# Moving the modulation products of a two-layer transformer kernel to VectorE, and attention splits to GpSimd

## What is computed

```python
def modulation(cond, w_mod, b_mod):            # cond (1024,), w_mod (1024, 6144)
    return jnp.split(jax.nn.silu(cond) @ w_mod + b_mod, 6, axis=-1)

h   = x * (1.0 + sc1) + sh1                    # then a mixer, then
x   = layer_norm(ALPHA * x + gt1 * o, ...)
h   = x * (1.0 + sc2) + sh2                    # then a gated feed-forward
x   = layer_norm(ALPHA * x + gt2 * f, ...)
```

## Time and profile before

| | |
|---|---|
| median of three runs | 2785.85 us (2783.92 to 2786.07) |
| the profiled execution | 2784.94 us, its span 2782.8 us |
| busy share of the span | PE 97%, DVE 50%, ACT 36%, POOL 2% |
| window attention of layer 0 | 126 to 240 us |
| first feed-forward, gate/up of the first half | 495 to 693 us |
| its down tiles; its second half | 693 to 795 us; 795 to 973 us |
| heads of differential attention, 17 us each | 1249 to 1380 us |

### The profile page before, as it was taken

The page is one execution under the profiler, slowest core; times in us unless marked ns, Lnnn a source line. Parts: engine busy times, 40 slices in busy tenths (PEclk is TensorE's granted clock), DMA queues, the critical chain, the costliest instruction groups (busy, mean ns, idle before and its releaser), DMA issues.

```text
span 2782.8 us, 41495 instructions
## 1 busy us (share of the span) xinstructions
PE 2704.5 (97%) x17620; PEld 2230.9 (80%) x17620; DVE 1383.0 (50%) x2453; ACT 1014.9 (36%) x1636; POOL 66.7 (2%) x54
## 2 busy tenths in 40 slices
PE   7999999999999999999999999999989999999999
PEld 5876678888888887877788888887766887888887
DVE  3377544434344535427757636459567434433333
ACT  3355543322112227536634323342256222332221
POOL 2000000100000001000001002000000000000000
PEclk9999999999999999999999999999989999999999
DMA  6332010222433331210012332311310223222322
GB/s 263 114 119 70 26 39 31 76 101 93 141 130 113 112 100 54 66 56 8 1 62 77 105 107 91 107 59 64 116 57 9 99 98 95 80 91 88 110 85 89
DMA packets 67351, 236.64 MB, mean 85 GB/s; under 512 B 7392, under 2 KB 10592, under 8 KB 66528
## 3 DMA queue, kind: packets, MB, share of 16 engines
q1 hardware_dynamic: 66592, 231.38, 24.5%
q10 hardware_dynamic: 576, 2.62, 0.3%
HBM read 231.87 MB, written 2.10 MB: 84 GB/s over the span
## 4 chain that ended last, share of the span: by engine, by line
PE 90%; DVE 6%; ACT 2%; issue 1%; DMA 1%; SPq 0%; DVEq 0%; ACTq 0%
PE PSA L695 87%; PE PSA L1010 2%; PE PSA L1281 1%; DVE stat L3197 1%; DVE WS L2363 1%; DMA Y<-in_early 1%; DVE Y L3188 0%; DMA W<-in_weights 0%; PE PSA L1635 0%; ACT WS L1736 0%; DVE HS L2540 0%; ACT Y L2205 0%; DVE YS L2363 0%; DVE PSA L3196 0%; DVE X L2478 0%
## 5 line engine op out<-in xcount | busy, mean ns | idle before, releaser
L695 PE MATMUL PSA<-HS,WS 128*128 128x512 f32 (+1 forms) x6480 | 1300.8, 361 | 11.1 <-DVE HS L2540 5.1
L695 PEld LDWEIGHTS PSA<-HS,WS 128*128 128x128 f32 x6480 | 1091.4, 189 | 209.3 <-issue 12.1
L2363 DVE TENSOR_TENSOR WS<-W,WS 128x1024 fp32r<-128x1024 f32 (+2 forms) x313 | 357.6, 1145 | 622.7 <-ACT WS L1736 622.1
L1736 ACT ACTIVATE WS<-W 128x1024 fp32r<-128x1024 f32 (+2 forms) x313 | 307.8, 986 | 738.9 <-PE PSA L695 369.7
L695 PE MATMUL PSA<-YS,WS 128*128 128x512 f32 (+1 forms) x2232 | 469.6, 372 | 4.1 <-DVE YS L3221 3.5
L695 PEld LDWEIGHTS PSA<-YS,WS 128*128 128x128 f32 x2232 | 393.0, 189 | 78.4 <-DVE YS L3221 3.9
L695 PE MATMUL PSA<-Y 128*64 128x128 f32 (+9 forms) x2368 | 286.5, 342 | 18.1 <-ACT Y L1887 6.5
L695 PEld LDWEIGHTS PSA<-Y 128*64 128x64 f32 (+3 forms) x2368 | 174.3, 151 | 97.0 <-issue 65.9
L695 PE MATMUL PSA<-HS,YS 128*128 128x512 f32 (+1 forms) x696 | 125.6, 337 | 0.4 <-DVE X L2471 0.4
L695 PEld LDWEIGHTS PSA<-HS,YS 128*128 128x128 f32 x696 | 106.6, 189 | 16.1 <-issue 2.3
L2687 DVE TENSOR_TENSOR Y<-Y,PSA 128x512 f32<-128x512 f32 (+1 forms) x66 | 51.2, 776 | 125.2 <-PE PSA L695 117.1
(11 more groups left out here) (353 smaller groups left out, 2291.4 us busy)
## 6 DMA issues: line engine op xcount, KB each, us to landing
W<-in_weights SPq DMA_DIRECT2D x391, 512.0 KB, 3.3
Y<-in_early SPq DMA_DIRECT2D x4, 2048.0 KB, 18.8
W<-in_weights SPq DMA_DIRECT2D x24, 256.0 KB, 2.6
X<-in_x SPq DMA_DIRECT2D x4, 768.0 KB, 20.1
W<-in_weights SPq DMA_DIRECT2D x24, 128.0 KB, 2.3
Y<-in_ssm ACTq DMA_DIRECT2D x1, 1024.0 KB, 7.2
out<-X SPq DMA_DIRECT2D x1, 1024.0 KB, 4.6
C<-in_consts SPq DMA_DIRECT2D x1, 884.5 KB, 30.2
```

The costliest lines, as they stand in the source:

```text
L695: return pe.matmul(out, lhsT, rhs, start=first, stop=last)
L1736: act.activation(split_home(n)[:, 0, 0:f], W[:, c % W_RING, 0:f], ACT.Copy)\
L2363: tt(home[:, 1, 0:f], W[:, c % W_RING, 0:f], home[:, 0, 0:f].bitcast(F32), ALU.subtract)\
```

## The change

**Modulation.** `ROWS` lists 80 row chunks in place of 32: tiles 40 to 47 of layer 0 and 0 to 15 of layer 1, each once for each condition row (the product overwrites the chunk, so it is loaded twice), and tiles 16 to 47 of layer 1 once. `row_tiles` deals them out over the same 29 steps, two or three to a step (22 steps have three). No modulation product is left on PE in the feed-forward, and window attention has them only at n = 1 to 15 (n = 16 has the last sums). There, ACT copies the products to `MT` behind its exponential, and DVE adds the bias ahead of its row maximum. `COND` has two rows; it lies over the masks, cosines and sines, `MT` and `silu_c`, is loaded after window attention, and its silu stands at m = 0. 

**Splits.** In both attentions of layer 0, GpSimd makes hi and lo of the output (`split_outputs`); only for the last unit of latent attention does DVE. PE waits for them ahead of the output projection; after window attention it waits for the drained PSUM tile (L2611) alone. In differential attention, GpSimd splits queries and keys of heads 1 to 7 (`split_head`: five pieces of 256 columns, a copy and a subtraction each), and their scores are three fp32r matmuls in place of one float32 matmul. Head h is split from the time at which head h-2 has its last scores (heads 1 and 2 from the end of the value products).

```diff
+ROWS = ([(0, n, s) for n in range(40, 48) for s in range(2)] + [(1, n, s) for n in range(16) for s in range(2)]
+        + [(1, n, 0) for n in range(16, 48)])
...
-    for n in range(1, 24):
-        step(("swa", n), 0, 1)
-    for half, ms in halves():
...
-    step(("ffn", 1, True, 0), 1, 0)
+    for n in range(1, 17):
+        step(("swa", n), 0, 1 if n < 16 else 0)
...
-                        if f == 0:
-                            if turned_chunks(half, m):
-                                modulation(("ffn", half, False, m))
...
+                if h and i == t == 0:
+                    pe.wait_ge(heads_split, value("heads_split", h))
                 for c, j, nj in score_runs(u):
...
+                    if h == 0:
+                        ins = mm(out, QD[r, h, tokens], KDf[r, h, keys], True, True)
+                    else:
+                        q, k = head_parts(h)
+                        ins = products(out, (q[r, 0, tokens], q[r, 1, tokens]), (k[r, 0, keys], k[r, 1, keys]), True, True)
...
+                            if t and (u[0], n) in m_index and msteps[m_index[u[0], n]][2]:
+                                m = m_index[u[0], n]
+                                _, products = mod_columns(m)
+                                ins = act.activation(MT[:, m % 2, 0:P], PS[slot(key)][:, products:products + P], ACT.Copy)
...
+                        if f == 0 and m == 0:
+                            act.wait_ge(rows_landed, 16)
+                            act.activation(COND[:], COND[:], ACT.Silu).then_inc(rows_ready, one("rows_ready"))
...
+            def split_outputs(units, first_tile):
+
+                for u in units[1::2]:
+                    key = out_job(u)
+                    plain, hi, lo = output_home(u, first_tile)
+                    pool.wait_ge(psum_drained[slot(key)], turn(key))
+                    link(pool.tensor_copy(hi, plain))
+                    pool.tensor_tensor(lo, plain, hi.bitcast(F32), ALU.subtract)\
+                        .then_inc(outputs_split, one("outputs_split", key))
+                pool.wait_ge(outputs_split, value("outputs_split", key))
...
+            def split_head(h):
+
+                if h < 3:
+                    pool.wait_ge(psum_filled[slot(("dv", 1, 2))], turn(("dv", 1, 2)))
+                else:
+                    for t in range(2):
+                        last = (DIFF_UNITS[4 * (h - 2) + 3], "scores", t)
+                        pool.wait_ge(psum_filled[slot(last)], turn(last))
+                pool.wait_ge(rope_done, value("rope_done", ("dk", h)))
+                for src, dst, pieces in zip((QD[:, h, :], KDf[:, h, :]), head_parts(h), (2, 3)):
+                    for c in range(pieces):
+                        cols = slice(2 * P * c, 2 * P * (c + 1))
+                        link(pool.tensor_copy(dst[:, 0, cols], src[:, cols]))
+                        ins = pool.tensor_tensor(dst[:, 1, cols], src[:, cols], dst[:, 0, cols].bitcast(F32), ALU.subtract)
+                ins.then_inc(heads_split, one("heads_split", h))
...
-            def row_modulation(ns):
+            def row_modulation(tiles_):
...
+                    w = W[:, w_slot(*chunk), :]
+                    stt(w, w, 1.0, COND[:, s, :], ALU.mult, ALU.mult, accum_out=MOD[:, layer, m, s:s + 1])\
                         .then_inc(rows_multiplied, one("rows_multiplied", n))
```

More of the change, by code:

```diff
@@ L72, in ff_chunks @@
             if f == 0:
-                w += [("mod", 1, n) for n in mod1_chunks(half, m)]
+                w += [("mod",) + r for r in row_tiles(half, m)]
         for m in range(KD):
@@ L76, in ff_chunks, with row_tiles @@
             if f == 0:
-                w += [("mod", 1, n) for n in mod1_chunks(half, m, True)]
+                w += [("mod",) + r for r in row_tiles(half, m, True)]
     return w
-def mod1_chunks(half, m, down=False):
+def row_tiles(half, m, down=False):
     if down:
@@ L86, in mod1_chunks @@
         step = m - 1 if half == 0 else m - 1 + KD
[L87 to L98, removed]
+    steps_, n = MF - 1 + KD, len(ROWS)
+    return [] if step is None or step < 0 else ROWS[n * step // steps_:n * (step + 1) // steps_]
 IN2 = ([("u", m) for m in range(4)] + [("cb", m) for m in range(4)]
@@ L146, in plan_weights @@
     w += [("even_in", 9)] + [("mod", 0, EARLY + n) for n in (7, 8)]
-    w += [("mod", 0, n) for n in range(EARLY + 9, 48)] + [("w_qb", 0), ("w_qb", 1), ("w_kvb",)]
+    w += [("mod", 0, n) for n in range(EARLY + 9, 40)] + [("w_qb", 0), ("w_qb", 1), ("w_kvb",)]
     w += [("mix0", m) for m in range(KD)] + ff_chunks(0)
@@ L298, in build @@
         heads_rounded = sem("heads_rounded")
+        heads_split = sem("heads_split")
         shared_key_spread = sem("shared_key_spread")
@@ L454, in build, with head_parts @@
         SQD = part(Y, 20224, S)
+        def head_parts(h):
+            at = 2560 * (h % 2)
+            return part(HS, at, 2, S), part(HS, at + 2 * S, 2, T)
         ROT1 = part(Y, 17152, 2, S)
@@ L1927, in feed_forward @@
                         more_weights(("up", f, m))
+                        if f == 0 and m == 0:
+                            act.wait_ge(rows_landed, 16)
+                            act.activation(COND[:], COND[:], ACT.Silu).then_inc(rows_ready, one("rows_ready"))
                         if f == 0 and m:
-                            more_weights(("mod", 1, mod1_chunks(half, m)[-1]))
-                        if f == 0 and m == 2:
-                            act.wait_ge(rows_landed, 16)
-                            act.activation(COND, COND, ACT.Silu).then_inc(rows_ready, one("rows_ready"))
+                            more_weights(("mod",) + row_tiles(half, m)[-1])
                         if f == 1 and m == 5:
@@ L2334, in modulation, with keep_sums @@
                 return key, ins
+            def keep_sums(where, ps):
+                n = m_index[where]
+                sums, _ = mod_columns(n)
+                _, layer, done = msteps[n - 1]
+                a, c = done[0], len(done)
+                tt(MOD[:, layer, a:a + c, :], ps[:, sums:sums + 2 * c].rearrange("p (c s) -> p c s", s=2),
+                   par("b_mod", 48 * layer + a, c).unsqueeze(2).broadcast_to((P, c, 2)), ALU.add)
             def ring_modulation(where):
@@ L2418, in residual @@
                 for m in range(4 if ahead else KD):
-                    mods = mod1_chunks(0, m, True) if key == ("down", 0, 0) else range(0)
-                    where = ("ffn", key[2], True, m) if key[0:2] == ("down", 0) else None
+                    row_of = row_tiles(0, m, True) if key == ("down", 0, 0) else []
                     if m in ahead:
```

115 lines of the change are left out of this document (56 added, 59 removed).

## The result

The changed kernel took 2791.65 us (median of 7 runs, 2789.93 to 2798.58) beside 2785.34 us of the kernel before on the same chip (7 runs, 2781.66 to 2786.07). The ratio, estimated from all runs, is 1.0034, 95% interval 1.0025 to 1.0044: slower by 0.34%, about 9.5 us, where 17.6 us less had been predicted. The two medians alone are 6.3 us apart, a little less than the interval's lower end, and the spans of the two profiled executions 6.4 (2789.2 us against 2782.8). All of them say slower; how much is known to some 3 us.

What follows compares the result with a forecast made beforehand. PE, busy 97% of the span, was taken as the bound unless DVE, GpSimd or the weight ring came last; gains of 8.2 (window attention), 4.9 (feed-forward) and 4.5 (differential attention) summed to 17.6 us: median 2768, range 2760 to 2775.

Steps and rivals of the forecast that it cites:

- The ring: First feed-forward: weight chunk c loads when c-4 is consumed; added rows delay later chunks, 6.9 us of stalls in all.
- the down steps at 0.6 us each: Feed-forward down steps: next first chunk ready at 12.8 to 13.9 against 12.65; 0.6 in five steps, 3 us.
- the turn at 2: Turn from gate/up to down: PE's 0.54 us stall for L2659 grows by 1.6 to 2.5, taken as 2 us.
- the gate/up steps at 0.1: Feed-forward gate/up steps: from nothing to 0.7 us late, taken as 0.1 over 15 three-row steps, 1.5 us.
- the 11.8 predicted for the removed tiles: First feed-forward: modulation tiles and sums leave PE, 11.8 us less on a PE without gaps.
- behind three rows: Down step: next tile's first chunk, issued at 6.5 us, lands at 10.5 to 11.6, ready at 12.8 to 13.9.
- The clock: Prediction is wrong if PE's granted clock, 0.97 in window attention, falls to its lower level more often at new gaps.
- The first rival: Feed-forward: each of 22 three-row steps stalls 0.7 us, the stage loses 3.6; whole kernel 2777 us; chance 0.17.
- The slower one: Feed-forward: load hanging on the first row lands after 6.2 us, not 3.2; 2.2 us lost per step, 2809; chance 0.06.
- predicted at 8.2 us: Window attention: removed modulation tiles 4.1 and 1.2 us, shorter waits at n = 6, 12, 18 and the end; 8.2 gained.
- 6.2 - 1.7 = 4.5 us: Differential attention: fp32r score pairs gain 0.22 us each, 6.2 in 28; GpSimd's contention with DVE costs 1.7.
- if two such streams don't overlap: Differential attention's other bound: fp32r streams on array halves run one after another, a pair takes 2.1 us, a loss of 5.

Runs made afterwards that it cites:

- 7: The changed kernel with 24 two-row tiles loaded once, the ratio of condition rows made early, their second products cut to 8 columns: 2760.96 us, ratio 0.992.
- 4: The kernel before with GpSimd splitting differential attention's heads and both attentions' outputs, all modulation tiles still on PE: 2776.03 us, ratio 0.9975.
- 1: The changed kernel with 24 two-row tiles loaded once and multiplied twice, the second time by the ratio of the rows: 2781.9 us, ratio 0.9994.
- 6: The changed kernel with the 24 second-row products and their chunk loads cut to 8 columns, order of 80 transfers kept: 2766.74 us, ratio 0.9947.
- 3: The kernel before with differential attention's change alone (heads 1 to 7 split by GpSimd, scores from the split parts): 2780.29 us, ratio 0.9992.
- 11: The kernel before with GpSimd's head splits running but scores still from the unsplit values: 2782.35 us, ratio 0.9996.
- 8: The changed kernel, two-row tiles loaded once, ratio made early, the turn's last gate tile split ahead of row products: 2770.36 us, ratio 0.9954 (0.9953 without that reordering).
- 12: The changed kernel, two-row tiles loaded once, ratio made early, double products moved to gate/up steps, first-layer bias added at its last product: 2762.87 us, ratio 0.9928.

## Why the prediction was wrong

**The ring, the step that failed.** The prediction took the down steps at 0.6 us each, the turn at 2 and the gate/up steps at 0.1: 6.9 us of stalls. Without stalls the first half takes 172.86 us (7), 12.6 less than before, close to the 11.8 predicted for the removed tiles. Against that and the other two stretches of before, after loses 6.4 + 19.5 + 6.8 = 32.7 us, in place of the 6.9. The term that was mis-sized is the landing of the next first chunk "behind three rows": issued at 6.5 and landing at 10.5 to 11.6, 4.0 to 5.1 us later. Issued at 701.25 it took 6.6 us, and at 715.00 7.29. In a step of three rows, all chunks from one second chunk to the next first one (issue to landing by the trace, us):

| chunk | issued | landed | us |
|---|---|---|---|
| second of the down tile, alone | 726.86 | 729.41 | 2.56 |
| row | 728.00 | 731.38 | 3.38 |
| row | 729.15 | 734.87 | 5.73 |
| row | 729.52 | 736.12 | 6.60 |
| first of the next down tile | 730.82 | 737.37 | 6.55 |

I had read the 6.2 us of the earlier trace rows as 3.2 and 1 us for each chunk ahead. Near that is only the spacing of a pair that is issued 0.4 us apart (1.25 us here between landings); the second row, issued 1.15 us behind the first, lands 3.5 us behind it, and all that follow are late with it. The trace of before had this already: a row issued at 696.52, 1.15 us behind another, landed 5.44 us later. The landing was mis-sized by some 2 us, and the ring had next to no slack. (The pair that "ended at 731.85" is the first chunk's lo part and then that of the second; the first, which PE wants at 731.6, was done at 731.25, so 0.35 us were left.) Had the prediction taken its own 6.2 of the earlier trace rows for this chunk, it would have been ready at 6.5 + 6.2 + 1.06 + 1.23 = 15.0 against 12.65; the trace has 15.08 from residual to residual.

The same term failed at the turn: the chunk ahead of L2659 was given 4.2 us from issue to landing, took 6.12 (from 684.49), and PE stood 5.04 us in place of 2 or 3. In the gate/up steps the next gate chunk was given 3.3 to 4.5 us; in the steps with three rows that I followed (590 to 680 and 816 to 912 us) it took 3.9 to 5.8. The prediction had "from nothing to 0.7" a step and took 0.1, 1.5 us in all; it was 6.4 + 6.8 = 13.2 us over 20 steps, of which PE's waits show 3.7 + 4.4; where the other 5 us lie within PE's busy time was not traced. The count of chunks was off as well: this stage carries 80 modulation chunks in place of 48, 32 more and not 24; the 24 are the whole kernel's, which loads eight fewer in window attention.

**The clock** was named as what would make the prediction wrong and was given no price. Behind the stalls of 5.0 and 2.25 us in the down stretch PE's own work took up to 4.3 us longer. On the chain it was less: PE stands there for 2.30 us behind the first stall, half of which a full clock would have saved, and not at all behind the second. The ring, and not the clock, made the loss.

**The rivals.** The first rival (every step of three rows stalls 0.7 us, the stage loses 3.6) named the right place, with a size too small. The slower one, given 0.06, named the load that hangs on the first row. That was the wrong chunk: the second chunk of the down tile lands after 2.56 us, as predicted. The late one is the chunk behind the rows. In effect the outcome is between the two: 32.7 us over 22 steps is 1.5 a step, just past the 1.4 from which the prediction would have called the kernel slower.

**Window attention** was predicted at 8.2 us, and 8.65 came, of which 1.07 were there at its first maximum already, so 7.6. The split of it roughly stands: 3.1 for the output splits (4), where the prediction has 2.9 in the waits at n = 6, 12 and 18 and at the end, and 4.4 for the tiles, where it has 4.1 + 1.2. PE's granted clock in the window fell from 0.97 to 0.94: it was at its lower level for 13.7 us in after and for 6.8 before. In 1 and 6, with the same program up to there and 10.2 us at that level, the first up product comes 2 us sooner than in after. So the agreement to half a microsecond is luck: the sum had no term for the clock, and traces of one program differ here by more than that. That the 2 us are the clock's alone is not shown.

**Differential attention** was predicted at 6.2 - 1.7 = 4.5 us; 2.8 came (3: 2.9). Both terms were off, in opposite directions. Contention cost nothing on the path that the traces tell from scatter (11: 151.43 us beside 151.19) in place of 1.7, and the chain of after from 1326 to 1344 us runs over PE alone. The scores of a unit gained 0.11 and not 0.22 us: a head went from 17.06 to 16.63 us. PE's timeline in after:

```profile
1320.51 1.90 PE L693 MATMUL PSA<-HS 64*128 64x512 f32 x12
1322.34 0.87 PE L1281 MATMUL PSA<-C,Y 128*128 128x128 f32 x6
1323.05 1.50 PE L693 MATMUL PSA<-X,Y 128*128 128x128 f32 x12
1324.48 1.88 PE L693 MATMUL PSA<-HS 64*128 64x512 f32 x12
1326.30 0.87 PE L1281 MATMUL PSA<-C,Y 128*128 128x128 f32 x6
```

From the first score to the turning that follows the pair of score tiles takes 1.82 us, where I had 1.35. At the 0.352 us that 768 columns take in the feed-forward, their six products would take 2.11 us one after another and 1.06 side by side: the halves of the array overlapped only a little. That was nearly the case "if two such streams don't overlap". It didn't become the loss of 5 that I gave it, because the pair is 1.82 and not 2.1, under float32's 1.50 and 2.35 by turns (counted in the same way in the trace of before), 1.93 on average. That difference is the 0.11.

## What to carry to other kernels

Where weights stream through a short ring, write the ring as a cycle (consume, issue in the queue's order, land, round, split, consume) and compare its length with PE's step, for each kind of step. If they are equal already, products, chunks and bytes put into it lengthen the step, however idle the engine and however low the DMA share: 48 products and 32 chunks cost 32.7 us here with DVE busy for 51% and a DMA share of 0.41. It isn't a price for each that adds up: leaving out 24 products of 1.15 us gave back 14.4 us, and only 8.6 once the loads were fewer. Put the added work into the steps whose PE time is longest, and don't load a tile twice for two products: with both, and the silu moved ahead, the same products went from 9.5 us slower to 20 us faster than before. A releaser in a trace names the last of several waits; only removing it (8) tells whether it is the one that counts.

## What the runs showed of the hardware that I had not expected

- A reciprocal on VectorE of 128x1024 float32 took 6.55 us, a product of the same shape 1.23.
- 512 KB transfers of one queue in after: alone 3.1 to 3.4 us from issue to landing; issued 0.4 us apart they land some 1.25 us apart; one issued 1.15 us behind another landed 3.5 us after it (5.73 from its issue). The fourth of a burst took up to 7.29.
- fp32r matmuls on the two halves of the array, 12 of them in 1.82 us, overlapped only a little (2.11 us one after another, 1.06 side by side, by the feed-forward's rate), where eight float32 records took 1.57 us at best. Whether that holds for such matmuls outside this stage was not tried.
- GpSimd's splits beside VectorE's combination cost that 0.11 us of 1.02 on average.
- A PE stall of 5.0 us was followed by 6.83 us at the lower clock (5.2 of them after its end), one of 2.25 us by 3.41 us. In 12 the stall of 3.2 us at the turn was followed by 3.4 us at it, and the granted clock over that stretch was 0.99.
